# Moving the second layer's S5 parameters into the end of the first layer, and splitting half of one input projection

## What is computed

```
h = rms_norm(x, norm_g)
proj = jnp.einsum('bsd,de->bse', h, w_in)            # 1024 -> 10008 columns
u_lru, u_s5, qkv_ret, q_nsa, kv_nsa, bg_nsa, gate_paths, merge = split_columns(proj, IN_SIZES)
...
ys = ys * jax.nn.silu(gate_paths.reshape(bsz, s, N_BRANCH, BRANCH_W))
branch = jnp.einsum('bsnw,nwd->bsnd', ys, w_branch)
merged = jnp.sum(jax.nn.sigmoid(merge.reshape(bsz, s, N_BRANCH, d)) * branch, axis=2)
return x + jnp.einsum('bsd,de->bse', merged, w_out)
```

```
dt = jnp.exp(log_dt)[:, None];  lr = jnp.minimum(lam_re, -1e-4)
mag = jnp.exp(lr * dt);  ab_re = mag * jnp.cos(li * dt);  ab_im = mag * jnp.sin(li * dt)
f_re = (nr * lr + ni * li) / den;  f_im = (ni * lr - nr * li) / den      # nr = ab_re - 1, ni = ab_im
```

## Time and profile before

| | us |
|---|---|
| runs shown (3) | 749.69, 751.04, 751.25; median 751.04 |
| profiled execution | 749.62 |
| its span | 747.8 |
| PE busy | 734.8 (98%) |
| PEld / DVE / ACT / POOL busy | 623.7 / 486.2 / 421.2 / 307.4 |

### The profile page before, as it was taken

One profiled execution on the slowest core, in us unless ns is written; L12 is line 12 of the kernel. 1 busy time (PEld: TensorE's weight loads), 2 busy tenths in 40 slices (PEclk: granted clock), 3 DMA queues, 4 the chain that ended last, 5 costly groups with the idle time before them and its releaser, 6 DMA issues.

```text
span 747.8 us, 14583 instructions
## 1 busy us (share of the span) xinstructions
PE 734.8 (98%) x6014; PEld 623.7 (83%) x6014; DVE 486.2 (65%) x786; ACT 421.2 (56%) x676; POOL 307.4 (41%) x135
## 2 busy tenths in 40 slices
PE   8999999999999999999989999999999999999996
PEld 7888898889888888878888878988898788888785
DVE  5989977675685634535688799767565947153344
ACT  7885635538464655544558664444476345655442
POOL 3000000035977976688100000000647979766750
PEclk9999999999999999999999999999999999999999
DMA  8669637553553655555545875665625456545541
GB/s 261 188 197 272 218 124 226 185 180 114 159 151 115 196 147 144 164 173 167 150 95 169 283 190 172 202 201 187 200 85 169 134 149 175 168 137 170 172 137 56
DMA packets 87009, 126.85 MB, mean 170 GB/s; under 512 B 22072, under 2 KB 32672, under 8 KB 86944
## 3 DMA queue, kind: packets, MB, share of 16 engines
q1 hardware_dynamic: 86624, 125.63, 55.9%
q10 hardware_dynamic: 320, 0.30, 0.1%
HBM read 124.86 MB, written 1.05 MB: 168 GB/s over the span
## 4 chain that ended last, share of the span: by engine, by line
PE 93%; DVE 3%; issue 2%; ACT 1%; DMA 0%; POOL 0%; SPq 0%; POOLq 0%; DVEq 0%; ACTq 0%
PE proj L1745 68%; PE M L1740 5%; PE proj L1782 4%; PE proj L1786 2%; PE proj L1813 2%; PE M L2140 2%; PE M L1942 1%; DVE sc L1556 1%; PE M L1953 1%; PE M L1910 1%; PE proj L1828 1%; PE proj L1844 1%; PE M L2114 1%; PE M L2017 1%; PE M L2109 1%
## 5 line engine op out<-in xcount | busy, mean ns | idle before, releaser
L698 POOL TENSOR_TENSOR w_lo<-raw,w_hi 128x1024 fp32r<-128x1024 f32 x112 | 291.4, 2633 | 391.8 <-ACT w_hi L720 368.7
L720 ACT ACTIVATE w_hi<-raw 128x1024 fp32r<-128x1024 f32 x200 | 206.5, 1054 | 108.8 <-PE proj L1745 64.8
L1745 PE MATMUL proj<-w_hi,h_hi 128*128 128x512 f32 x544 | 216.8, 399 | 0.0
L1745 PE MATMUL proj<-w_hi,h_lo 128*128 128x512 f32 x544 | 212.4, 390 | 0.0
L1745 PE MATMUL proj<-w_lo,h_hi 128*128 128x512 f32 x544 | 212.0, 390 | 0.0
L1745 PEld LDWEIGHTS proj<-w_hi,h_lo 128*128 128x128 f32 x544 | 102.1, 188 | 22.2 <-issue 0.5
L1745 PEld LDWEIGHTS proj<-w_hi,h_hi 128*128 128x128 f32 x544 | 102.2, 188 | 21.8 <-issue 0.9
L1745 PEld LDWEIGHTS proj<-w_lo,h_hi 128*128 128x128 f32 x544 | 102.3, 188 | 20.4 <-issue 0.5
L1329 DVE TENSOR_TENSOR w_lo<-raw,w_hi 128x1024 fp32r<-128x1024 f32 x80 | 95.0, 1221 | 27.0 <-ACT w_hi L720 19.5
L1745 PE MATMUL proj<-w_hi,ys_hi 128*128 128x512 f32 x128 | 51.0, 398 | 0.0
L1745 PE MATMUL proj<-w_hi,ys_lo 128*128 128x512 f32 x128 | 50.0, 391 | 0.0
(11 more groups left out here) (342 smaller groups left out, 1175.7 us busy)
## 6 DMA issues: line engine op xcount, KB each, us to landing
raw<-in_w_in SPq DMA_DIRECT2D x152, 512.0 KB, 4.3
raw<-in_w_branch SPq DMA_DIRECT2D x32, 512.0 KB, 4.0
raw<-in_w_out SPq DMA_DIRECT2D x16, 512.0 KB, 4.1
raw<-in_s_w_glu SPq DMA_DIRECT2D x8, 512.0 KB, 4.8
raw<-in_w_in SPq DMA_DIRECT2D x8, 256.0 KB, 3.0
merged<-in_nsa_ck_w SPq DMA_DIRECT2D x4, 512.0 KB, 6.9
mt<-in_nsa_ck_w SPq DMA_DIRECT2D x4, 512.0 KB, 8.9
merged<-in_nsa_cv_w SPq DMA_DIRECT2D x4, 512.0 KB, 4.6
```

Of the source, the lines that this page charges most:

```text
L698: nc.gpsimd.tensor_tensor(w_lo[:, slot(s, l), 0:n * w], raw[:, u % N_RAW, 0:n * w], w_hi[:, slot(s, l), 0:n * w].bitcast(f32), ALU.subtrac ...
L720: i = nc.scalar.activation(out_, in_, func, **kw)
L1745: last = mm(dst, left[i], right[j], start=start and n == 0, stop=stop and n == 2, skip_group_check=True)
```

## The change

For the second layer, the turn of the vectors and all of the S5 parameters move into the last part of the first layer. Units 2 and 3 of `u_lru` become split units in both layers, with the low parts on DVE.

```diff
-NATIVE = ("cmp", "u_lru")
+NATIVE_UNITS = [u for u in range(NU) if (CHUNKS[UNITS[u][0]][0], u - UNIT_END[UNITS[u][0] - 1]) in
+                [("cmp", n) for n in range(4)] + [("u_lru", n) for n in range(2)]]
...
-LO_ON_VECTOR = ("u_s5", "ret_v", ...
+LO_ON_VECTOR = ("u_s5", "u_lru", "ret_v", ...
 # ACT, start of a layer
                     run(bgate[:, :, :], cm[:, :, 256:CMP_W], ACT.Tanh, cmp_read, scale=0.5)
+                    cast_units(UNIT_END[CHUNK["u_lru"]])
                     keep_wT(0, 0)
 # ACT, end of a layer
                     cast_room("branch_nsa_0")
+                    if l + 1 < DEPTH:
+                        parameters_exp(l + 1)
                     for half in range(2):
                         act.wait_ge(mT_done, half + 1)
                         run(flat(h_hi[:, 4 * half:4 * half + 4, :]), ...
                         if not half:
                             cast_units(UNIT_END[CHUNK["branch_nsa_1"]] + N_SPLIT)
+                            if l + 1 < DEPTH:
+                                parameters_mag(l + 1)
+                                parameters_sin(l + 1)
 # DVE, start of a layer
                     if l == 0:
                         vector.wait_ge(const_loaded, 16)
-                    parameters_c(l)
-                    parameters_d(l)
+                        parameters_c(0)
+                        parameters_d(0)
...
                     make_v(0)
+                    split_lo("u_lru", 2, 3)
+                    split_lo("ret_v", 0)
                     make_v(1)
-                    split_lo("ret_v", 0, 1)
+                    split_lo("ret_v", 1)
 # DVE, end of a layer
                     lo_of_gated("nsa")
-                    branch("nsa", 0)
                     if l + 1 < DEPTH:
                         expand_dt(vector, l + 1)
+                        keep_vectors(vector, l + 1)
+                        parameters_a(l + 1)
+                    branch("nsa", 0)
+                    if l + 1 < DEPTH:
+                        parameters_e(l + 1)
                     for half in range(2):
                         if half:
                             branch("nsa", 1)
+                            if l + 1 < DEPTH:
+                                parameters_b(l + 1)
+                                parameters_c(l + 1)
+                                parameters_d(l + 1)
                         dve.wait_ge(mhi_done, half + 1)
                         v.tensor_tensor(flat(h_lo[...
 # PE, end of a layer
                     chunk("branch_nsa_0")
+                    if l + 1 < DEPTH:
+                        pe.wait_ge(no_cmp, 1)
+                        turn_vectors(tensor, l + 1)
                     chunk("branch_nsa_1", 0)
                     pe.wait_ge(mt_free, 5)
+                    if l + 1 < DEPTH:
+                        Layer(tensor, l + 1).wait_ge(vec_ready, 1)
                     blocks_T(0, merged[:, 0]).then_inc(mT_done, 1)
                     chunk("branch_nsa_1", 1)
```

More of the change, by code:

```diff
@@ L69 @@
 N_SPLIT = 5
-NATIVE = ("cmp", "u_lru")
-SPLIT_UNITS = [u for u in range(NU) if CHUNKS[UNITS[u][0]][0] not in NATIVE]
-LO_ON_VECTOR = ("u_s5", "ret_v", "nsa_kv", "gate_s5", "gate_lru", "merge_s5_0", "merge_s5_1", "ret_q", "ret_k", "nsa_q",
+NATIVE_UNITS = [u for u in range(NU) if (CHUNKS[UNITS[u][0]][0], u - UNIT_END[UNITS[u][0] - 1]) in
+                [("cmp", n) for n in range(4)] + [("u_lru", n) for n in range(2)]]
+SPLIT_UNITS = [u for u in range(NU) if u not in NATIVE_UNITS]
+LO_ON_VECTOR = ("u_s5", "u_lru", "ret_v", "nsa_kv", "gate_s5", "gate_lru", "merge_s5_0", "merge_s5_1", "ret_q", "ret_k", "nsa_q",
                 "out_0b", "out_1b")
@@ L106 @@
     "dec_ready": 2, "dt_exp": 1, "dt_rows": 1, "evacuated0": 16, "evacuated1": 16, "gate_tanh": 2, "h_done": 2,
-    "hfull_done": 8, "hhi_done": 8, "hi_done": 100, "hidT_done": 2, "hid_arg": 1, "hid_ready": 1, "hid_tanh": 1,
+    "hfull_done": 8, "hhi_done": 8, "hi_done": 102, "hidT_done": 2, "hid_arg": 1, "hid_ready": 1, "hid_tanh": 1,
     "hid_tm_ready": 2, "hlo_done": 8, "kcT_done": 1, "kcT_ready": 1, "kc_ready": 1, "kern_ready": 2, "kp_done": 2,
@@ L115 @@
     "v0_ready": 1, "v_ready": 2, "var": 2, "vbd_ready": 1, "vecT": 2, "vec_ready": 1, "vectors_loaded": 208,
-    "vk_ready": 2, "vlo_done": 44, "wT_done": 4, "wT_ready": 4, "w_ready": 2, "wbd_ready": 2, "wl_loaded": 64,
+    "vk_ready": 2, "vlo_done": 46, "wT_done": 4, "wT_ready": 4, "w_ready": 2, "wbd_ready": 2, "wl_loaded": 64,
     "xT_done": 4, "x_half": 3, "x_scaled": 4, "xc_ready": 1, "y_done": 2, "y_ready": 2, "yg_hi": 4, "yg_lo": 4,
@@ L1674, in _ @@
                     lo_of_gated("nsa")
+                    if l + 1 < DEPTH:
+                        expand_dt(vector, l + 1)
+                        keep_vectors(vector, l + 1)
+                        parameters_a(l + 1)
                     branch("nsa", 0)
                     if l + 1 < DEPTH:
-                        expand_dt(vector, l + 1)
+                        parameters_e(l + 1)
                     for half in range(2):
@@ L1684, in _ @@
                                         flat(h_hi[:, 4 * half:4 * half + 4, :]).bitcast(f32), ALU.subtract).then_inc(mlo_done, 1)
[L1685 to L1692, removed]
+                    split_lo("out_0b", 0, 1)
                     split_lo("out_1b", 0, 1)
@@ L1706, in _ @@
                                            ALU.mult, ALU.add).then_inc(x_half, 1)
-                    if l + 1 < DEPTH:
-                        parameters_b(l + 1)
-                    else:
+                    if l + 1 == DEPTH:
                         vector.wait_ge(g_loaded, 16)
@@ L1762, in chunk @@
                             _, k0, nk, _ = UNITS[u]
-                            if name in NATIVE:
+                            if u in NATIVE_UNITS:
                                 pe.wait_ge(raw_loaded[u % N_RAW], raw_target[u])
@@ L1787, in chunk @@
                                                       start=st_, stop=sp_, skip_group_check=True)
-                                elif name in ("gate_s5", "gate_lru"):
+                                elif name in ("u_lru", "gate_s5", "gate_lru"):
                                     for m in range(4):
@@ L2197, in _ @@
                     if l + 1 < DEPTH:
-                        Layer(tensor, l + 1).wait_ge(vec_ready, 1)
                         for t in range(TT):
```

5 lines of the change are left out of this document (removed).

## The result

The changed kernel takes 756.78 us, median of 4 runs (756.49 to 757.36), against 750.41 us for the kernel before in the same comparison. The ratio is 1.0093, with a 95% interval of 1.008 to 1.0105: slower by 0.9%, some 6.4 us. The profiled executions, 756.49 against 749.62, differ by 6.9 us, and so do the spans. I had forecast slower, at 754.9, that is 3.85 us above the 751.04 from which I started.

The account below looks back on a forecast made before the run. PE, busy 734.8 of 747.8 us, was taken to bound the kernel. The split's +0.70 and -0.75 and the moved parameters' +3.9 sum to +3.85 on the 751.04 median: 754.9 us, range 751.5 to 756.8.

Parts of the forecast that it names:

- The split, first layer: At u_lru unit 2, PE waits 1.67 us for DVE's low part, then saves 0.97 of its own work: +0.70 us.
- The split, second layer: At u_lru, PE saves 0.97 us without waiting, then waits about 0.2 at nsa_kv's low part: -0.75 us.
- The transposition: At merged[:, 0], first layer's end, POOL holds DVE's small operations, delaying PE by 4.2 us; +3.9 without the turn.
- That cover is 1.1 us thick.: Behind out_1a, b, c, d and the low parts finish 1.1 us before PE wants them, so they cost nothing.
- rival A: At the transposition the tensor_scalar is held by POOL, while later memsets hold nobody: 754.9 us, chance 0.30.
- A2: POOL's memsets also hold b's tensor_scalar, so PE waits about 1.5 us more at out_0b: 756.4 us, chance 0.22.
- B: At the transposition only two-input operations are held, costing 2.3 us in place of 3.9: 753.3 us, chance 0.19.
- C: At the transposition nothing is held, since small operations fall between POOL's; +0.6 us there, 751.6 in all, chance 0.18.
- D: PE does not wait for DVE at split or branch sum; only PE's saved work counts: 749.1 us, chance 0.08.

Follow-up runs that it names:

- experiment 3: Changed kernel with parameters_a on DVE moved behind the sum of branch(nsa, 0), keep_vectors still ahead of it; ratio 1.0079.
- experiment 7: Changed kernel with 12 matmuls of zeros on PE filling its 3.0 us wait before the transposition; span 754.0 us in one execution.
- experiment 12: Changed kernel with both the 12 matmuls of zeros in the 3.0 us wait and POOL's memsets behind DVE's second h_lo; 752.82 us, ratio 1.0044.
- experiment 4: Changed kernel with parameter parts b, c and d back where the kernel before has them; ratio 1.0068.
- experiment 2: Changed kernel without the split, so only the second layer's parameters are moved; ratio 1.0113.
- experiment 5: Changed kernel with POOL's two memsets put behind DVE's second h_lo; span 751.8 us in one execution.
- experiment 9: Changed kernel run once more, unchanged, for a second profile; span 754.7 us in one execution.
- experiment 8: Kernel before plus the split alone, with the low part of u_lru 2 computed inside make_v(0); 748.28 us, ratio 0.9985.
- experiment 6: Changed kernel with vectors turned and keep_vectors and a begun earlier, e behind branch(nsa, 1), mag, sin, b, c, d at old places; 749.75 us, ratio 1.0005.
- experiment 11: Kernel of experiment 8 with matmuls of zeros (6 and 2) filling PE's waits at the boundary between the layers; 748.67 us, ratio 0.9988.

## Why the prediction was too low

The direction and the mechanism at the transposition were right; the sum of +3.85 was missing 3 us.

- **The split, first layer.** +0.70 predicted, +0.65 measured: unit 2's low part is done at 43.5, and PE starts its 48 matmuls at 43.54 (43.44 predicted). They take 6.01 us, not 5.94. Two executions of one kernel differ here by up to 0.2 us (110.32 and 110.11 for the 240 matmuls of the changed kernel), so the agreement is no finer than that.
- **The split, second layer.** -0.75 predicted, -0.78 measured.
- **The transposition.** 352.5 predicted on the first layer's old clock, 353.2 with its +0.70, and 352.67 measured, by the mechanism that the prediction chose: a `tensor_scalar` held by POOL's running subtraction at the full price. It was the third operation of `a` and not the second, which passed at 0.16 us; since the hold ends with POOL's work, this changes nothing. The term in the sum was a little too large. I had written +4.2 against 348.32 and added the first layer's +0.70 beside it, but POOL's work shifts with the first layer, and the two share 0.65: the place costs 3.70, less the 0.27 us of the turn.
- **"That cover is 1.1 us thick."** This is the step that failed. It took the memsets to hold nobody (rival A). The memset holds the first `tensor_scalar` of `b` for 1.66 us there, 2.95 where DVE comes sooner (experiments 3 and 7), and A2's mechanism is the one that is true. At full clock its place is true too: PE waits 1.39 us at `out_0b` in experiment 7 where A2 had 1.5, and not at all in experiment 12, so without the memset the cover does hold. In the changed kernel the slow clock made PE late as well, and that wait was nothing in the first profile and 0.69 us in the second.
- **What neither A nor A2 has is the way to the end.** DVE's low parts of `out_0b` are late, and SP issues the next layer's first weights only behind the first of them. SP's row before, and now:

```profile
362.00 6.02 SPq L457 DMA_DIRECT2D raw<-in_w_in  x4
```

```profile
369.58 3.77 SPq L458 DMA_DIRECT2D raw<-in_w_in  x4
```

Their casts, their low parts and the sum into `x` queue behind that, and PE waits at the turn of `x`: 2.5 us where it had been 1.3. Moving the memsets alone brings the boundary back to that of experiment 4, and between experiments 7 and 12, both at full clock behind the transposition, it brings the first turn of `x` from 383.00 to 380.66 (the rest of the 3.0 us between their spans stands at the boundary, where only experiment 7 has the slow clock). So it is the memset and not the 5.3 us of `b`, `c`, `d` that breaks the cover. How far the lateness would go with a slow clock and no memset was not tried. A2's 756.4 lies near the 756.78 measured, but by luck in part: its sum has neither this path nor the clock.
- **The granted clock was in no term.** I counted PE's wait at its length. Behind such waits the clock fell to 0.50 in most profiled executions, three of five and eight of thirteen. In the changed kernel's first profile that was 1.57 us behind the transposition, of which the end saw 0.4 to 0.7 (experiment 7: 0.38 at the sum into `x`, 0.7 in the span), and 1.0 at the boundary.
- **Rivals B and C** are refuted by the 2.35 us of L1128, which recurred in experiments 2, 4, 5, 7, 9 and 12. **D** failed at its own condition: PE did wait for DVE, 1.6 us at the split and 3.0 at the transposition; experiment 8 reaches part of what it gives (1.0 us at the median), once the low part is ready when PE wants it.

Put together: 0.65 - 0.78 + 3.70 - 0.27 is 3.3, which experiment 12 measures as 3.2; then 2.7 for the held `b` and the clock that feeds it, and 1.0 for the clock at the boundary, is 6.9.

## What to carry to other kernels

Before small VectorE work is moved ahead of an operation on the critical path, lay GpSimd's timeline under the new place, memsets included. Here an instruction that is 0.16 us long by itself cost what was left of GpSimd's running instruction; moved by 12 us into a gap of GpSimd's, it was free to within what experiment 6 can tell. And when a stall is added, ask which buffer the stalled engine frees late: here the price came 20 us later, through buffers and transfers.

Work off the critical path gained nothing by being moved: PE had never waited for these parameters where they were. The one thing that paid, by 0.15%, was to put a low part ahead of work that nobody was waiting for (experiment 8).

## What the runs showed of the hardware

- A GpSimd memset holds a VectorE `tensor_scalar` of 128x16 for its whole remaining length (1.66, 2.66 and 2.95 us), across two memsets in a row, and lets `tensor_tensor` with two SBUF inputs pass at 0.16 to 0.17 us (experiment 6). With the memsets moved away the `tensor_scalar` took 0.16 us (experiments 5 and 12).
- The VectorE instruction right behind one that had been held got through, though GpSimd's next instruction followed at once (347.72, 0.16 us), and the one after it was held for 2.35 us. The same 0.68, 0.16 and 2.35 us stand in experiments 2, 4, 5, 7, 9 and 12. GpSimd then ran out of work, so whether a longer row would go on by turns is not shown.
- In the changed kernel, with waits at the boundary that agree to 0.06 us, the boundary took 1.00 us more in the execution in which the granted clock fell to 0.50 there than in the one in which it stayed at 1.00. In experiment 6 the ten spans form two groups some 1 us apart, and the upper four have a mean granted clock of 0.997 where the lower six have 0.998 or 0.999; where the clock fell in those without a profile is not known. The Trainium skill (TensorE: Matmul & The Clock Gate, What's actually happening) says that the hardware watches the array's activity on a beat of its own, which does not restart with the kernel, so that the moment of a change varies. The traces agree in that the moment varied; the beat itself they do not show.
- With a wait filled by matmuls of zeros the clock behind it was 1.00 in all three profiles (experiments 7, 11 and 12). Experiments 4 and 5 had it so at the transposition without filling, so it is not shown that the filling did it. In experiment 11, where other waits stayed open, the median did not fall.
